# Four rows of the attention projection moved into the Hyena stage of a hybrid diffusion step

## The reference

```python
h = x * (1.0 + sc1) + sh1
q, k, v, z_hy, gate_a, gate_b = jnp.split(h @ lp['w_in'], SPLITS, axis=-1)
...
hy = hyena_branch(z_hy, lp)      # x0 * (filter (*) (x1 * u) + bias * (x1 * u)), the filter applied by rfft / irfft
merged = jax.nn.sigmoid(gate_a) * (attn @ lp['w_pa']) + jax.nn.sigmoid(gate_b) * (hy @ lp['w_pb'])
x = layer_norm(DEEPNORM_ALPHA * x + g1 * (merged @ lp['w_out']), lp['ln1_g'], lp['ln1_b'])
```

## Time and profile before

| | |
|---|---|
| three runs, median | 2139.69 us (2132.16 to 2140.95) |
| profiled execution | 2136.87 us, its span 2135.1 us |
| TensorE busy in the span | 2038.7 us (95%) |
| VectorE / ScalarE / GpSimd busy | 1146.1 / 751.6 / 167.9 us |
| mean granted TensorE clock | 0.982 |

### The profile page before, as it was taken

How to read it: one execution, slowest core, us unless ns; L and a number is a source line. 1 busy time by engine, 2 the same in 40 slices (tenths; PEclk the granted TensorE clock), 3 DMA queues, 4 the chain that set the end, 5 groups by cost and what they waited for, 6 DMA issues and landing times.

```text
span 2135.1 us, 30297 instructions
## 1 busy us (share of the span) xinstructions
PE 2038.7 (95%) x13030; PEld 1931.2 (90%) x13030; DVE 1146.1 (54%) x1672; ACT 751.6 (35%) x1097; POOL 167.9 (8%) x190
## 2 busy tenths in 40 slices
PE   8999997999999999999999999799999999999997
PEld 3588886899989999999988888699999999999996
DVE  6415457866556767777544545763236443234335
ACT  3443444522245331233234434452225432123323
POOL 0120000100033000000022000010003200000011
PEclk9998998999999999999999999899999999999998
DMA  7331112244412344543322111212121211222111
GB/s 308 142 129 43 38 41 89 97 148 142 146 60 75 144 146 167 191 151 129 119 77 85 43 38 40 93 66 89 60 99 60 71 69 61 88 80 80 58 65 57
DMA packets 36862, 207.07 MB, mean 97 GB/s; under 512 B 4230, under 2 KB 7863, under 8 KB 18040
## 3 DMA queue, kind: packets, MB, share of 16 engines
q1 hardware_dynamic: 30904, 185.04, 24.4%
q0 software_dynamic: 2736, 13.35, 1.6%
q10 hardware_dynamic: 3088, 6.75, 0.8%
HBM read 196.98 MB, written 8.14 MB: 96 GB/s over the span
## 4 chain that ended last, share of the span: by engine, by line
PE 87%; DVE 5%; ACT 3%; issue 3%; DMA 1%; POOL 1%; SPq 0%; ACTq 0%; DVEq 0%; POOLq 0%
PE gemm_psum L571 51%; PE gemm_psum L601 14%; PE gemm_psum L621 4%; PE gemm_psum L639 3%; PE aux_psum L686 3%; PE gemm_psum L584 2%; PE aux_psum L737 2%; PE aux_psum L671 2%; PE gemm_psum L513 2%; PE gemm_psum L725 1%; PE gemm_psum L477 1%; DMA ada_early<-in_ada 1%; PE aux_psum L693 1%; ACT w_hi L1004 1%; PE aux_psum L497 1%
## 5 line engine op out<-in xcount | busy, mean ns | idle before, releaser
L571 PE MATMUL gemm_psum<-h_hi,w_hi 128*128 128x322 f32 x2176 | 505.6, 314 | 9.4 <-DVE gates L1747 3.9
L571 PE MATMUL gemm_psum<-h_hi,w_lo 128*128 128x322 f32 x2176 | 501.8, 312 | 0.0
L571 PE MATMUL gemm_psum<-h_lo,w_hi 128*128 128x322 f32 x2176 | 501.0, 311 | 0.0
L1440 DVE TENSOR_TENSOR w_lo<-w_raw,w_hi 128x2048 fp32r<-128x2048 f32 (+2 forms) x144 | 287.7, 1998 | 302.8 <-ACT w_hi L1004 301.1
L571 PEld LDWEIGHTS gemm_psum<-h_hi,w_hi 128*128 128x128 f32 x2176 | 369.2, 190 | 15.2 <-issue 10.8
L571 PEld LDWEIGHTS gemm_psum<-h_lo,w_hi 128*128 128x128 f32 x2176 | 369.3, 190 | 0.0
L571 PEld LDWEIGHTS gemm_psum<-h_hi,w_lo 128*128 128x128 f32 x2176 | 368.7, 190 | 0.0
L1004 ACT ACTIVATE w_hi<-w_raw 128x2048 fp32r<-128x2048 f32 (+2 forms) x144 | 239.6, 1664 | 170.6 <-PE gemm_psum L601 65.6
L1428 DVE CUSTOM_DVE_ANT_0 aux_psum<-w_raw,cond_by_row 128x1024 f32<-128x1024 f32 x160 | 191.0, 1256 | 6.4 <-DMA w_raw<-in_ada_t 6.2
L1557 DVE SCALAR_TENSOR_TENSOR x<-gemm_psum,mod,x 128x128 f32<-128x128 f32 (+2 forms) x144 | 55.3, 434 | 162.6 <-PE gemm_psum L601 129.3
L601 PE MATMUL gemm_psum<-act_hi,w_lo 128*128 128x322 f32 x616 | 141.9, 311 | 0.0
(11 more groups left out here) (296 smaller groups left out, 3192.7 us busy)
## 6 DMA issues: line engine op xcount, KB each, us to landing
w_raw<-in_w_up SPq DMA_DIRECT2D x44, 1024.0 KB, 4.8
w_raw<-in_ada_t SPq DMA_DIRECT2D x40, 1024.0 KB, 4.7
w_raw<-in_w_down SPq DMA_DIRECT2D x32, 704.0 KB, 4.2
w_raw<-in_w_gate SPq DMA_DIRECT2D x16, 1024.0 KB, 4.7
w_raw<-in_w_z SPq DMA_DIRECT2D x12, 1024.0 KB, 4.7
w_raw<-in_w_proj SPq DMA_DIRECT2D x16, 512.0 KB, 3.3
w_raw<-in_w_out SPq DMA_DIRECT2D x8, 1024.0 KB, 4.7
g_kept<-g_rows_out POOLq DMA_DIRECT2D x10, 512.0 KB, 2.9
```

Of the source, the lines that this page charges most:

```text
L571: last = mm(gp[:, 2 * (t % 2) + hf, 0:HALF], w[:, off + P * kk:off + P * (kk + 1)], moving(kk, lo)[:, hf * HALF:(hf + 1) * HALF], start=kk ...
L1440: TT(wlo[s][:, 0:n], raw[STEP[(lane.layer, "g", g)] % 2][:, 0:n], f32(whi[s][:, 0:n]), ALU.subtract).then_inc(sem["w_split"], raised("w_sp ...
```

## The change

It has five parts.

1. **A new chunk `pa`**, 2048 wide, holds the attention half of the projection weights for the first `EARLY` = 4 row blocks. Those four rows (24 matmuls of 322 columns each) are computed in the Hyena stage by `attn_projected` and copied by ScalarE to an SBUF buffer `attn_projected`, after being accumulated in whichever pair of PSUM banks is free. In the gate stage the blocks m < 4 have one projection tile in place of two; their projection chunk is 512 wide in place of 1024.
2. **Hyena on VectorE** reads the spectra directly in PSUM: ScalarE's ten copies per layer are gone, and the order of the products is changed so that each waits for one part only. `inverse` takes the imaginary part first, in the bank order 1, 2, 3, 0, with the wait for bank 0 ahead of that bank only.
3. **`g_spec` holds three pairs** in place of five; pairs 3 and 4 are fetched into the places of pairs 0 and 1 when these are used. The residues of the four latent blocks (`v_lo<-u_blocks`) move from VectorE to GpSimd.
4. **Splits and Hyena's end move.** ScalarE's split of the chunk I0 comes between the `y_hi` of pairs 0 and 1. `hy_hi` is made ahead of gate 0's sigmoids, ahead of the split of the first projection chunk.
5. **`ADA_SLOTS`** puts 0, 1, 1, 2, 2, 2, 2, 2 chunks of `w_ada` behind the eight gate chunks in place of 1, 2, 1, 2, 1, 2, 1, 2.

```diff
-        + [("F", 0), ("I", 0), ("F", 1), ("I", 1)]
+        + [("F", 0), ("pa", 0), ("I", 0), ("F", 1), ("I", 1)]
...
-    _n = 1 + _m % 2
+    _n = (0, 1, 1, 2, 2, 2, 2, 2)[_m]
...
-            gsp = sb("g_spec", [P, PAIRS, 2, HY_W], F32, s2)
+            gsp = sb("g_spec", [P, 3, 2, HY_W], F32, s2)
...
+    gA = gF + 1
+    gI, gF1, gI1, gG = gA + 1, gA + 2, gA + 3, gA + 4
+    chunk_done[gF:gG] = [("cinv_mm", 1), ("pa_mm", EARLY), ("linv_mm", 2), ("usp_mm", 10), ("linv_mm", 4)]
+    G_SLOT = [0, 1, 2, 0, 1]
+    EARLY_BANKS = [(1, 2), (1, 0), (1, 2), (0, 2)]
...   TensorE
+        def attn_projected(n):
+            s = slot_of(gA)
+            for kk in range(4):
+                for i, (w, a) in enumerate(((whi, ath), (whi, atl), (wlo, ath))):
+                    for hf in range(2):
+                        last = mm(early_bank(n, hf), w[s][:, P * (4 * n + kk):P * (4 * n + kk + 1)], a[:, kk, half(hf)],
+                                  start=kk == 0 and i == 0, stop=kk == 3 and i == 2)
+            last.then_inc(sem["pa_mm"], raised("pa_mm"))
...
-            pe.wait_ge(sem["w_split"], due("w_split", gF + 1))
-            for p_ in range(3):
+            pe.wait_ge(sem["pads_at"], due("pads_at", 1))
+            pe.wait_ge(sem["w_split"], due("w_split", gA + 1))
+            attn_projected(0)
+            pe.wait_ge(sem["us_ready"], due("us_ready", 1))
+            pe.wait_ge(sem["ut_out"], due("ut_out", 2))
+            spectrum(0, U_V[0])
+            pe.wait_ge(sem["ut_out"], due("ut_out", 5))
+            attn_projected(1)
+            for p_ in range(1, 3):
...
             last.then_inc(sem["cinv_mm"], raised("cinv_mm"))
-            pe.wait_ge(sem["cinv_out"], due("cinv_out", 1))
-            pe.wait_ge(sem["w_split"], due("w_split", gF + 2))
-            inverse(1, slot_of(gF + 1), True, False)
+            attn_projected(2)
+            pe.wait_ge(sem["usp_out"], due("usp_out", 4))
+            attn_projected(3)
+            pe.wait_ge(sem["w_split"], due("w_split", gI + 1))
+            pe.wait_ge(sem["pa_out"], due("pa_out", 3))
+            inverse(1, slot_of(gI), True, False)
...
-                tile(g + 1, 0, 4, 0, lambda kk, lo: (atl if lo else ath)[:, kk, :], "proj_mm")
+                if m >= EARLY:
+                    tile(g + 1, 0, 4, 0, lambda kk, lo: (atl if lo else ath)[:, kk, :], "proj_mm")
...   ScalarE
+            early_row(0)
+            u_hi(5, 9)
+            early_row(1)
             for p_ in range(PAIRS):
-                for o in range(2):
-                    r = 2 * p_ + o
-                    act.wait_ge(sem["usp_mm"], due("usp_mm", r + 1))
-                    if p_:
-                        act.wait_ge(sem["y_ready"], due("y_ready", 2 * p_))
-                    run(us[:, o, :], gp[:, r % 4, :], ACT.Copy).then_inc(sem["usp_out"], raised("usp_out"))
...
+                if p_ == 0:
+                    split(gI)
                 if p_ == 1:
-                    split(gF + 2)
+                    early_row(2)
+                    early_row(3)
+                    split(gF1)
...   GpSimd
+            for n in range(5, 9):
+                pool.wait_ge(sem["us_hi"], due("us_hi", n + 1))
+                G.tensor_tensor(vlo[:, US_V[n], :], ureg[:, n - 5, :], f32(vhi[:, US_V[n], :]), ALU.subtract)\
+                    .then_inc(sem["us_rest"], raised("us_rest"))
```

More of the change, by code:

```diff
@@ L58 @@
 NG = len(GEMM)
-WIDTH = {"q": 2048, "k": 1024, "v": 1024, "z": 2048, "gate": 2048, "proj": 1024, "out": 2048,
+EARLY = 4
+WIDTH = {"pa": EARLY * 512, "q": 2048, "k": 1024, "v": 1024, "z": 2048, "gate": 2048, "proj": 1024, "out": 2048,
          "up": 2048, "down": DOWN_W}
-WG = [g for g in range(NG) if GEMM[g][0] not in "FI"]
+WG = [g for g in range(NG) if GEMM[g][0] not in ("F", "I")]
 def width(g):
@@ L67, in width @@
         return (F0_BLOCKS, F1_BLOCKS)[i] * P
-    return CHUNK if kind == "I" else WIDTH[kind]
+    return CHUNK if kind == "I" else 512 if kind == "proj" and i < EARLY else WIDTH[kind]
 def stream():
@@ L142, with proj_i @@
 H_FFN, H_NEXT = 2 * KD, 4 * KD
+def proj_i(m, c):
+    return m + 1 if m < EARLY else EARLY + 2 * (m - EARLY) + c + 1
 def half(h):
@@ L299, in _program @@
             sb("u_blocks_space", [P, 4, HY_W], F32, s2)
-            yhi = sb("y_hi", [P, 2, 2, HY_W], F32R, s2)
+            early = sb("attn_projected", [P, EARLY, ROW], F32, s2)
     with ExitStack() as s:
@@ L375, in _program @@
     for g, (kind, i) in enumerate(GEMM):
-        for c in range({"F": 0, "I": 0, "k": 1, "v": 1, "down": 1}.get(kind, 2)):
+        for c in range(1 if kind == "proj" and i < EARLY else
+                       {"F": 0, "I": 0, "pa": 0, "k": 1, "v": 1, "down": 1}.get(kind, 2)):
             TILES.append((g, c))
@@ L386, in _program @@
     for kind, i in GEMM:
-        if kind in "FI":
+        if kind in ("F", "I", "pa"):
             chunk_done.append(None)
@@ L398, in _program @@
             ev = kind + "_mm"
-            n_of[ev] = n_of.get(ev, 0) + 2
+            n_of[ev] = n_of.get(ev, 0) + (1 if kind == "proj" and i < EARLY else 2)
             chunk_done.append((ev, n_of[ev]))
@@ L451, in _ @@
                 src, w = A["w_" + GEMM[i][0]][L, GEMM[i][1]], width(i)
+                if GEMM[i][0] == "proj" and GEMM[i][1] < EARLY:
+                    src = src[:, w:2 * w]
             sp.dma_start(raw[n % 2][:, 0:w], src).then_inc(sem[f"raw{n % 2}"], 16)
@@ L731, in inverse @@
             ys = Y_SLOT[pair_]
-            pe.wait_ge(sem["y_ready"], due("y_ready", 2 * pair_ + 2))
-            for j in range(NHY):
-                for o in range(2):
+            for o in (1, 0):
+                pe.wait_ge(sem["y_ready"], due("y_ready", 2 * pair_ + 2 - o))
+                for j in (1, 2, 3, 0):
+                    if first and o and j == 0:
+                        pe.wait_ge(sem["cinv_out"], due("cinv_out", 1))
                     at = 512 * (2 * ((pair_ - 1) % 2) + o)
@@ L737, in inverse @@
                         last = mm(ax[:, j, :], y[:, ys, o, P * j:P * (j + 1)], w[slot][:, at:at + 512],
-                                  start=first and o == 0 and n == 0, stop=final and o == 1 and n == 2)
+                                  start=first and o == 1 and n == 0, stop=final and o == 0 and n == 2)
             last.then_inc(sem["linv_mm"], raised("linv_mm"))
@@ L1149, in _ @@
                     soft(i)
-            split(gF + 1)
-            act.wait_ge(sem["z_mm"], due("z_mm", 12))
+            split(gA)
             def u_block(b):
@@ L1170, in _, with early_row @@
             u_hi(1, 5)
-            for p_ in range(PAIRS):
-                for o in range(2):
-                    r = 2 * p_ + o
-                    act.wait_ge(sem["usp_mm"], due("usp_mm", r + 1))
-                    if p_:
-                        act.wait_ge(sem["y_ready"], due("y_ready", 2 * p_))
-                    run(us[:, o, :], gp[:, r % 4, :], ACT.Copy).then_inc(sem["usp_out"], raised("usp_out"))
-                if p_ == 0:
-                    u_hi(5, 9)
+            def early_row(n):
+                act.wait_ge(sem["pa_mm"], due("pa_mm", n + 1))
+                run(two(early[:, n, :]), early_pair(n), ACT.Copy).then_inc(sem["pa_out"], raised("pa_out"))
+            early_row(0)
+            u_hi(5, 9)
+            early_row(1)
+            for p_ in range(PAIRS):
                 for o in range(2):
@@ L1201, in _ @@
                 run(hhi[:, d, :], hsrc[:, d % 2, :], ACT.Copy).then_inc(sem["h_hi"], raised("h_hi"))
-            split(gF + 5)
+            for j in range(NHY):
+                hi(hyh[:, j, :], xu[:, j, :], "hy_src", j + 1, "hy_hi")
+            split(gG + 1)
             for m in range(KD):
@@ L1212, in _ @@
                     run(two(gates[:, c, :]), pair(t), ACT.Sigmoid).then_inc(sem["gate_out"], raised("gate_out"))
-                if m == 0:
-                    for j in range(NHY):
-                        hi(hyh[:, j, :], xu[:, j, :], "hy_src", j + 1, "hy_hi")
                 split(g + 2)
@@ L1745, in _ @@
                     dve.wait_ge(sem["gate_out"], due("gate_out", 2 * m + c + 1))
-                    dve.wait_ge(sem["proj_mm"], due("proj_mm", 2 * m + c + 1))
-                    TT(two(gates[:, c, :]), two(gates[:, c, :]), pair(TILES.index((g + 1, c))), ALU.mult).then_inc(sem["proj_out"], raised("proj_out"))
+                    if m < EARLY and c == 0:
+                        dve.wait_ge(sem["pa_out"], due("pa_out", m + 1))
+                        TT(gates[:, 0, :], gates[:, 0, :], early[:, m, :], ALU.mult).then_inc(sem["dve_order"], raised("dve_order"))
+                        continue
+                    dve.wait_ge(sem["proj_mm"], due("proj_mm", proj_i(m, c)))
+                    TT(two(gates[:, c, :]), two(gates[:, c, :]), pair(TILES.index((g + 1, c if m >= EARLY else 0))), ALU.mult)\
+                        .then_inc(sem["proj_out"], raised("proj_out"))
+                dve.wait_ge(sem["dve_order"], now("dve_order"))
```

102 lines of the change are left out of this document (57 added, 45 removed).

## The result

The changed kernel takes 2119.2 us in the median of its runs, against 2132.6 us in the median of six runs of the kernel before. The ratio is 0.9926, with a 95% interval from 0.9906 to 0.9947: 11 to 20 us saved, where 16.9 us had been worked out. One of the six runs, at 2482 us, was disturbed and is left out of the ratio. The profiled execution took 2114.95 us with a span of 2113.1 us, 22.0 us shorter than the span before.

What follows compares the result with a forecast made beforehand. TensorE, busy 95% of the span, was taken as the bound, with idle holes and slow clock to save. Layer 1's 5.7 us plus layer 0's 11.2 us make 16.9 us, giving 2123 us; range 2116 to 2130, eight in ten 2110 to 2136.

Steps and rivals of the forecast that it cites:

- The walk through the Hyena stage: Hyena stage, each layer: 14.3 us of projection taken in for 1.3 us, so gate 0 starts at 1400.6 instead of 1399.29.
- the sign named for being right: Start of gate 0, counted from the start of the Hyena stage: 1 to 3 us later than before.
- The third rival: Hyena stage: the ScalarE to VectorE chain becomes the bound, hand-overs late, 4 us per layer, 2131 us; chance 0.11.
- the slower one: Hyena stage: TensorE stays at 1.2 GHz throughout, up to 27.6 us added per layer, 2178 us; chance 0.05.
- Row 0: First moved projection row, opening the Hyena stage: costs between 3.6 and 7.2 us depending on the clock, taken as 5.2 us.
- The end of Hyena: Between gate 0 and gate 1: 2.6 us idle ahead of the Hyena tile, gate 1 starting 0.3 us later.
- Blocks 1 to 3: Gate stage: each block takes 19.45 us, not 17.85, held by a weight split; 2.0 us saved three times, 6.0 us.
- The first rival: Gate stage: splits served sooner, three blocks save the whole 3.6 us each, 9.6 us more, 2113 us; chance 0.08.
- The second rival: New short gaps: the clock falls behind three 1.6 us gaps per layer, 1.65 us each, 9.9 us, 2133 us; chance 0.14.
- the named signs of being wrong: Wait above 1 us before inverse 1 or spectrum 3, gate blocks 17.9 us apart, late `w_raw`, or clock 0.50 beyond 4 us.

## Why the prediction was right

The saving and the mechanism came out as forecast: 16.9 us were worked out, and 11 to 20 us measured, with 18.7 us in the two stages of the profiled executions. That the time itself, 2119.2 us, lies so near to the 2123 us named owes something to luck: the median of the kernel before had been 2139.7 us in the three runs that the forecast started from and is 2132.6 us in six, from which the same 16.9 us would give 2115.7 us. By its own steps:

- **The walk through the Hyena stage.** Gate 0 was to start 1.3 us later than before, counted from the stage's start. By PE's timeline it started 1.5 us later in layer 1 (63.4 us against 61.9) and 0.25 us earlier in layer 0 (61.85 against 62.1), where row 0 ran at full clock; there the sign named for being right, 1 to 3 us later, failed, on the good side. The order of what is late also held: the split of I0 waited for the context's inverse (5.71 us on ScalarE), `y_hi` stood behind it, and VectorE ended the split of F1 at 1357.25, PE asking at 1357.99, which is the 0.7 us to spare:

```profile
1345.28 1.92 ACT L1050 ACTIVATE w_hi<-w_raw 128x2048 fp32r<-128x2048 f32 x1 [5.71 <-PE aux_psum L868]
1347.11 1.13 ACT L1054 ACTIVATE y_hi<-u_spec 128x512 fp32r<-128x512 f32 x2
```
```profile
1348.96 2.28 DVE L1489 TENSOR_TENSOR w_lo<-w_raw,w_hi 128x2048 fp32r<-128x2048 f32 x1
...
1354.96 2.29 DVE L1489 TENSOR_TENSOR w_lo<-w_raw,w_hi 128x2048 fp32r<-128x2048 f32 x1 [2.69 <-ACT w_hi L1050]
```
  The third rival (the chain of ScalarE and VectorE bounds the stage) fell, and so did the slower one (the clock at 1.2 GHz through the stage). Its sum has a slip: 8.5 us of added time per layer only use up the gain; to be slower by the 10.7 us that can be told, it takes 13.8 us.
- **Row 0.** I took 5.2 us. In layer 1 it was 5.35, in layer 0 3.67. Behind the same gap of 2.72 us the clock fell in 3 of the 10 layers profiled with it, so 3.7 was the likelier value and 5.2 the exception, and layer 1's agreement with the 5.2 us is luck in this execution. In layer 0 gate 0 came 1.5 us sooner by it and gate 1 still 0.9 us; that is the largest part of why layer 0 gained 12.7 us and not 11.2.
- **The end of Hyena.** Forecast were 2.6 us of idle time ahead of the Hyena tile and gate 1 starting 0.3 us later; the rows say 2.17 us and, in layer 1, no later (84.6 us from the stage's start in both kernels). So gate 1 waited 0.73 us there and not at all in layer 0, where 1 to 2 us had been named as a sign.
- **Blocks 1 to 3** were to last 19.45 us; they last 19.51, and halving the weights brings 17.88. The first rival, weights in time, fell; with that edit it comes true.
- **Part 5** was priced at 5.5 us from two rows 1007.07 us apart. Alone it gives 5.4, taken out of the changed kernel it costs 6.5.
- **GpSimd** was forecast at 1.6 us a step and 0 to 1.9 us on VectorE, hidden. The steps took 1.4 us each, the side effect was 1.8, and it was hidden.
- **The second rival**, the clock falling in the new short gaps, came in part. It never fell behind the gaps of 1.36 us that I had priced, but behind the 2.17 us ahead of the Hyena tile it fell in 8 of the 12 layers profiled with that gap. The price is small: the tile takes 1.5 us more, gate 1 then has its weights in time, and from the tile's start to gate 1's 5.2 us pass instead of 4.6. One of the named signs of being wrong, the clock at 0.50 beyond the first 4 us, did appear with it in layer 0.

One part of the difference between the two profiled spans is not the change's: from the start of a layer's projections to the Hyena stage, layer 0 took 4.9 us less (217.0 to 212.1) and layer 1 3.7 us more (198.1 to 201.8). The last section shows why.

## What to carry to other kernels

Work that is moved into a hole is worth what it fills; what it leaves behind is worth only what the next bound allows. Here four tiles of 3.6 us were taken from the gate blocks and 2.0 us of three of them came through, because the tile had covered a weight split that can begin only when the whole slot is free; splitting by halves, each as soon as its own reader is done, gave the rest. Before a step is put beside others on GpSimd, or VectorE's order is tightened, look at what runs on the other of the two at that moment: a gap that is VectorE's dense work can be partly GpSimd's.
